# Expert rows scattered by choice and token, read back with plain loads, and summed on TensorE with diagonal matrices

## The reference

```python
    g_p, g_idx = lax.top_k(g_probs, 1)                       # the best of 4 groups
    ...
    e_p, e_idx = lax.top_k(e_probs, TOP_K)                   # the two best of its 8 experts
    e_p = e_p / jnp.sum(e_p, axis=-1, keepdims=True)
    weights = g_p * e_p
    expert_ids = g_idx * EXPERTS_PER_GROUP + e_idx
    ...
    a = jax.nn.silu(jnp.einsum('sd,edf->sef', xs, w_gate)) * jnp.einsum('sd,edf->sef', xs, w_up)
    return jnp.einsum('sef,efd->sd', a * cw[..., None], w_down)
...
        x = x + gt2[:, None, :] * ffn
    ...
    return modulate(rmsnorm(x, norm_f_g), sh_f, sc_f, dt)
```

## Time and profile before

| | us |
|---|---|
| median of 3 runs | 1380.87 |
| lowest, highest | 1378.67, 1381.21 |
| span of the profiled execution | 1383.9 |
| TensorE busy in the span | 1155.6 (84%) |
| VectorE busy | 659.2 (48%) |
| ScalarE busy | 324.7 (23%) |
| GpSimd busy | 138.1 (10%) |

### The profile page before, as it was taken

How to read it: one execution, slowest core, us unless ns; L and a number is a source line. 1 busy time by engine, 2 the same in 40 slices (tenths; PEclk the granted TensorE clock), 3 DMA queues, 4 the chain that set the end, 5 groups by cost and what they waited for, 6 DMA issues and landing times.

```text
span 1383.9 us, 16773 instructions
## 1 busy us (share of the span) xinstructions
PE 1155.6 (84%) x6596; PEld 936.1 (68%) x6596; DVE 659.2 (48%) x1390; ACT 324.7 (23%) x601; POOL 138.1 (10%) x211
## 2 busy tenths in 40 slices
PE   1589969999899989898978999729999999999700
PEld 1367958898789879796965444328888888888500
DVE  3744553362536666766762333462333333333286
ACT  1434261134314453344332111220000000000021
POOL 0000100000000000000000000142111111110083
PEclk9999985589756989999888999868999999999955
DMA  9301420032200513232177342525899898896172
GB/s 344 116 1 31 144 70 0 1 92 66 87 1 0 164 50 110 89 92 77 42 249 285 134 143 92 206 55 172 336 333 334 331 333 334 331 332 257 52 272 86
DMA packets 86861, 216.03 MB, mean 156 GB/s; under 512 B 18400, under 2 KB 47120, under 8 KB 78480
## 3 DMA queue, kind: packets, MB, share of 16 engines
q1 hardware_dynamic: 61152, 148.41, 30.6%
q0 software_dynamic: 13664, 50.26, 11.1%
q10 hardware_dynamic: 11984, 16.54, 3.4%
HBM read 194.70 MB, written 32.93 MB: 164 GB/s over the span
## 4 chain that ended last, share of the span: by engine, by line
PE 73%; DVE 13%; DMA 4%; ACT 4%; issue 2%; ACTq 2%; POOL 0%; POOLq 0%; SPq 0%; DVEq 0%
PE PS L1731 17%; PE PS L1682 8%; PE PS L1738 8%; PE PS L1599 7%; PE PS L1554 7%; PE PS L1555 7%; PE PS L1556 6%; PE PS L1614 2%; DVE X L1488 2%; PE PS L1723 2%; PE PS L1525 2%; PE PS L1616 2%; DMA WF<-in_w_in 2%; PE PS L1602 2%; PE PS L1600 1%
## 5 line engine op out<-in xcount | busy, mean ns | idle before, releaser
L1731 PE MATMUL PS<-XGT,WGU 128*128 128x96 f32 x2048 | 236.8, 277 | 0.0
L1731 PEld LDWEIGHTS PS<-XGT,WGU 128*128 128x128 f32 x2048 | 235.3, 194 | 0.5 <-issue 0.5
L1554 PE MATMUL PS<-WH,HT 128*128 128x256 f32 x512 | 151.8, 297 | 2.6 <-ACT FD L785 1.6
L1555 PE MATMUL PS<-WL,HT 128*128 128x256 f32 x512 | 150.6, 294 | 0.0
L1556 PE MATMUL PS<-WH,HL 128*128 128x256 f32 x512 | 150.4, 294 | 0.0
L1599 PE MATMUL PS<-XL 64*128 64x128 f32 (+1 forms) x640 | 120.9, 356 | 9.3 <-ACT KH L864 5.7
L1599 PEld LDWEIGHTS PS<-XL 64*128 64x128 f32 (+1 forms) x640 | 113.9, 269 | 12.3 <-ACT KH L864 10.9
L1171 DVE COPY_PREDICATED AT<-MASK,PS 128x64 f32<-128x64 uint8 x320 | 72.7, 227 | 100.1 <-PE PS L1602 81.4
L1682 PE MATMUL PS<-WOUT,OT 128*128 128x512 f32 x256 | 113.4, 602 | 3.5 <-DVE H2T L1277 3.3
L1738 PE MATMUL PS<-WDN,ATT 128*96 128x512 f32 x256 | 115.0, 592 | 0.0
L1554 PEld LDWEIGHTS PS<-WH,HT 128*128 128x128 f32 x512 | 104.7, 204 | 3.9 <-DVE WL L1071 2.2
(11 more groups left out here) (258 smaller groups left out, 1652.5 us busy)
## 6 DMA issues: line engine op xcount, KB each, us to landing
WGU<-in_w_exp_gate SPq DMA_DIRECT2D x32, 1024.0 KB, 8.3
WGU<-in_w_exp_up SPq DMA_DIRECT2D x32, 1024.0 KB, 11.1
WDN<-in_w_exp_down SPq DMA_DIRECT2D x32, 1024.0 KB, 5.0
AR<-in_w_ada POOLq DMA_DIRECT2D x32, 512.0 KB, 4.3
WF<-in_w_in SPq DMA_DIRECT2D x28, 512.0 KB, 5.4
expert_rows<-YB ACTq DMA_DIRECT2D x32, 384.0 KB, 8.6
AST<-in_w_ada SPq DMA_DIRECT2D x16, 512.0 KB, 12.2
AR<-in_w_ada_final POOLq DMA_DIRECT2D x16, 512.0 KB, 3.8
```

What stands on the lines that cost most here:

```text
L1554: MM(ps, wh, xh, start=first, stop=False)
L1555: MM(ps, wh, xl, start=False, stop=False)
L1731: last = MM(GU[par][:, col:col + C], WGU[slot][:, m, k, j * P:(j + 1) * P], XGT[:, par, k, :], start=(k == 0), stop=(k == KD - 1))
```

## The change

1. `ys_d` is no longer laid out by expert slot but as planes of rows by token: choice 0 of token j in row j, choice 1 in row 2048 + j (`PLANE` is 2T = 2048). The table holds this row number (`TID` has one column more, for k); its low 11 bits are the token. Empty slots hold 7168, which a bounds check leaves out both as a token number (its low 11 bits are 1024) and as a row.
2. After `IDX` is read, VectorE masks it into `IDXG` (token numbers) in one instruction, and the gathers use that.
3. The stores on ScalarE are gone. GpSimd scatters the 96 rows of `YB` by the column of `IDX` (`scatter`), in its loop ahead of the gather of the expert seven further on.
4. The fill of the extra slices is gone.
5. ScalarE writes 16 diagonal 128x128 matrices `DIAG[k, t]` with the tokens' weights `WPAIR` when the down projection of expert 29 is done.
6. In the last stage SP loads both rows of each token of a tile with one plain DMA of 1 MB, four tiles deep; TensorE makes four 512-column matmuls per tile, which weight and sum the two rows in PSUM; VectorE adds that to `X1`, two tiles ahead of the norm, and adds the shift itself. GpSimd has no part in it.

```diff
-    FILL = -(-NX * C // NT)
+    PLANE = 2 * T
+    PAD = 7 * T
...
-        ys_d = nc.dram_tensor("expert_rows", [NSLOT, D], F32, kind="Internal").ap()
+        ys_d = nc.dram_tensor("expert_rows", [PLANE + T, D], F32, kind="Internal").ap()
...
+            for s in range(2):
+                sp.wait_ge(y_st[s], 16 * NE // 2)
+            sp.wait_ge(extras_done, 1)
+            ys_rows = ys_d.rearrange("(k t p) d -> p k t d", p=P, t=NT)
+
+            def load_rows(t):
+                sp.dma_start(YG[:, t % 4, :, :], ys_rows[:, 0:3:2, t, :]).then_inc(yg_in[t % 4], 16)
+
+            for t in range(4):
+                load_rows(t)
             for t in range(NT):
+                if t + 4 < NT:
+                    sp.wait_ge(ysum_ready, t + 1)
+                    load_rows(t + 4)
                 sp.wait_ge(out_ready, t + 1)
                 sp.dma_start(out_rows[:, t, :], OUTT[:, t % 2, :]).then_inc(out_st[t % 2], 16)
...
-            nc.gpsimd.memset(ZT[:], T).then_inc(zt_ready, 1)
+            nc.gpsimd.memset(ZT[:], PAD).then_inc(zt_ready, 1)
...
-            pool.iota(TID[:], [[P, NT]], base=0, channel_multiplier=1).then_inc(ios, 1)
+            pool.iota(TID[:], [[PLANE, 2], [P, NT]], base=0, channel_multiplier=1).then_inc(ios, 1)
...
-            for t in range(NT):
-                pool.wait_ge(pj_ready, number[("wo", t, 0)] + 1)
-                lo, hi = FILL * t, min(FILL * (t + 1), NX * C)
-                pool.dma_start(ys_d[NE * C + lo:NE * C + hi, :], x[0, 0:hi - lo, :]).then_inc(ys_filled, 16)
...
-            pool.wait_ge(idx_in, 16)
+            pool.wait_ge(idxg_ready, 1)
...
+            def scatter(n, par):
+                pool.wait_ge(y_ev, n + 1)
+                nc.gpsimd.tensor_copy(IDXS[:, par:par + 1], IDX[:, bass.ds(n, 1)]).then_inc(idxs, 1)
+                pool.wait_ge(idxs, n + 1)
+                nc.gpsimd.tensor_tensor(TICK[:], IDENT[:, 0:1], IDENT[:, 0:1], ALU.add)
+                pool.indirect_dma_start(
+                    out=ys_d, out_offset=bass.IndirectOffsetOnAxis(ap=IDXS[:, par:par + 1], axis=0),
+                    in_=YB[0:C, par, :], in_offset=None,
+                    bounds_check=PLANE + T - 1, oob_is_err=False).then_inc(y_st[par], 16)
+
             for s in range(4):
                 gather(0, s, True)
-            with pool.Fori(1, NE // 4) as it:
+            for s in range(4):
+                if s == 3:
+                    scatter(0, 0)
+                gather(1, s, False)
+            with pool.Fori(2, NE // 4) as it:
                 for s in range(4):
+                    scatter(4 * it + (s - 7), (s + 1) % 2)
                     gather(it, s, False)
+            for n in range(NE - 7, NE):
+                scatter(n, n % 2)
...
-            def shift(t):
-                pool.wait_ge(out_scaled, t + 1)
-                nc.gpsimd.tensor_tensor(OUTT[:, t % 2, :], OUTT[:, t % 2, :], SHF[:], ALU.add).then_inc(out_ready, 1)
-
-            for t in range(NT):
-                if t >= 4:
-                    pool.wait_ge(x2_ready, t - 3)
-                for k in range(2):
-                    pool.indirect_dma_start(
-                        out=YG[:, t % 4, k, :], out_offset=None, in_=ys_d,
-                        in_offset=bass.IndirectOffsetOnAxis(ap=SLOT[:, k, t:t + 1], axis=0)).then_inc(yg_in[t % 4], 16)
-                if t >= 4:
-                    shift(t - 4)
-            for t in range(NT - 4, NT):
-                shift(t)
...
-            def store(m, par, row):
-                act.wait_ge(y_ev, m + 1)
-                act.dma_start(ys_d[bass.ds(row, C), :], YB[0:C, par, :]).then_inc(y_st[par], 16)
...
+            act.wait_ge(y_ready, NE - 2)
+            for k in range(2):
+                for t in range(NT):
+                    last = A(DIAG[:, k, t, :], IDENT[:], ACT.Copy, scale=WPAIR[:, k, t:t + 1])
+            last.then_inc(diag_ready, 1)
...
+            v_.wait_ge(idx_in, 16)
+            V.tensor_single_scalar(IDXG[:], IDX[:], PLANE - 1, op=ALU.bitwise_and).then_inc(idxg_ready, 1)
...
             def add_rows(t):
-                for k in range(2):
-                    if k == 0:
-                        v_.wait_ge(yg_in[t % 4], 32 * (t // 4 + 1))
-                    i = V.scalar_tensor_tensor(out=X1[:, t, :], in0=YG[:, t % 4, k, :], scalar=WPAIR[:, k, t:t + 1],
-                                               in1=X1[:, t, :], op0=ALU.mult, op1=ALU.add)
...
+                v_.wait_ge(ysum_ready, t + 1)
+                V.tensor_tensor(X1[:, t, :], X1[:, t, :], YS[t % 2], ALU.add).then_inc(x2_ready, 1)
 
             add_rows(0)
+            add_rows(1)
             for t in range(NT):
-                if t + 1 < NT:
-                    add_rows(t + 1)
+                if t + 2 < NT:
+                    add_rows(t + 2)
...
+                v_.wait_ge(out_scaled, t + 1)
+                V.tensor_tensor(OUTT[:, t % 2, :], OUTT[:, t % 2, :], SHF[:], ALU.add).then_inc(out_ready, 1)
...
+            pe.wait_ge(diag_ready, 1)
+            for t in range(NT):
+                pe.wait_ge(yg_in[t % 4], 16 * (t // 4 + 1))
+                if t >= 2:
+                    pe.wait_ge(x2_ready, t - 1)
+                for half in range(2):
+                    hs = slice(half * HALF, (half + 1) * HALF)
+                    for k in range(2):
+                        last = MM(YS[t % 2][:, hs], DIAG[:, k, t, :], YG[:, t % 4, k, hs], start=(k == 0), stop=(k == 1))
+                last.then_inc(ysum_ready, 1)
```

More of the change, by code:

```diff
@@ L63, in layer_kernel @@
     NSLOT = (NE + NX) * C
-    FILL = -(-NX * C // NT)
+    PLANE = 2 * T
+    PAD = 7 * T
+    assert T & (T - 1) == 0
     GLA_UNITS, HG_UNITS = 2, 4
@@ L321, in layer_kernel @@
         SLOT = at("SLOT", 205.5625, [P, 2, NT], U32)
-        TID = at("TID", 205.625, [P, NT], U32)
+        TID = at("TID", 205.625, [P, 2, NT], U32)
+        IDXG = at("IDXG", 201.0, [C, NE + NX], U32)
         IDX = at("IDX", 200.5, [C, NE + NX], U32)
         IDXC = at("IDXC", 200.75, [C, 4], U32)
+        IDXS = at("IDXS", 200.78125, [C, 2], U32)
         XE = at("XE", 200.8125, [1, NX], I32)
@@ L330, in layer_kernel @@
         OUTT = at("OUTT", 64, [P, 2, D])
+        DIAG = at("DIAG", 136, [P, 2, NT, P])
         PS = ctx.enter_context(nc.psum_tensor("PS", [P, 8 * HALF], F32))
@@ L340, in layer_kernel @@
         YP = [PS[:, (4 + 2 * i) * HALF:(6 + 2 * i) * HALF] for i in range(2)]
+        YS = YP
         xn_d = nc.dram_tensor("xn_rows", [T, D], F32, kind="Internal").ap()
@@ L430, in layer_kernel @@
         extras_done = sem("extras_done")
-        ys_filled = sem("ys_filled")
+        idxs = sem("idxs")
+        idxg_ready = sem("idxg_ready")
+        xidxs = sem("xidxs")
+        diag_ready = sem("diag_ready")
+        ysum_ready = sem("ysum_ready")
         yg_in = [sem(f"yg_in{s}") for s in range(4)]
@@ L610, in _ @@
                             out=tab_d, out_offset=bass.IndirectOffsetOnAxis(ap=SLOTP[:, k, t:t + 1], axis=0),
-                            in_=TID[:, t:t + 1], in_offset=None, bounds_check=NSLOT - 1,
+                            in_=TID[:, k, t:t + 1], in_offset=None, bounds_check=NSLOT - 1,
                             oob_is_err=False).then_inc(table_st, 16)
@@ L631, in gather @@
                     pool.wait_ge(t_ready, 4 * it + (s - 3))
-                nc.gpsimd.tensor_copy(IDXC[:, s:s + 1], IDX[:, bass.ds(4 * it + s, 1)]).then_inc(idxc, 1)
+                nc.gpsimd.tensor_copy(IDXC[:, s:s + 1], IDXG[:, bass.ds(4 * it + s, 1)]).then_inc(idxc, 1)
                 pool.wait_ge(idxc, 4 * it + (s + 1))
@@ L649, in _ @@
                         pool.wait_ge(x_done, 16 * i + 16)
-                        nc.gpsimd.tensor_copy(IDXC[:, 0:1], IDX[:, bass.ds(i + NE, 1)]).then_inc(xidx, 1)
+                        nc.gpsimd.tensor_copy(IDXC[:, 0:1], IDXG[:, bass.ds(i + NE, 1)]).then_inc(xidx, 1)
                         pool.wait_ge(xidx, i + 1)
@@ L656, in _ @@
                             bounds_check=T - 1, oob_is_err=False).then_inc(xxg_in, 16)
-                pool.nop()
-            for s in range(2):
-                pool.wait_ge(y_st[s], 16 * NE // 2)
-            pool.wait_ge(extras_done, 1)
-            pool.wait_ge(ys_filled, 16 * NT)
-            def shift(t):
-                pool.wait_ge(out_scaled, t + 1)
-                nc.gpsimd.tensor_tensor(OUTT[:, t % 2, :], OUTT[:, t % 2, :], SHF[:], ALU.add).then_inc(out_ready, 1)
-            for t in range(NT):
-                if t >= 4:
-                    pool.wait_ge(x2_ready, t - 3)
-                for k in range(2):
-                    pool.indirect_dma_start(
-                        out=YG[:, t % 4, k, :], out_offset=None, in_=ys_d,
-                        in_offset=bass.IndirectOffsetOnAxis(ap=SLOT[:, k, t:t + 1], axis=0)).then_inc(yg_in[t % 4], 16)
-                if t >= 4:
-                    shift(t - 4)
-            for t in range(NT - 4, NT):
-                shift(t)
+                        pool.wait_ge(xyev, i + 1)
```

(19 more changed lines are left out.)

9 lines of the change are left out of this document (1 added, 8 removed).

## The result

The changed kernel takes 1368.95 us, the median of four runs (1367.32 to 1372.58), against 1380.78 for the kernel before on the same chip (1378.67 to 1381.21, four runs): ratio 0.9918, 95% interval 0.99 to 0.9935. The forecast was 1368.6 us, in a range of 1363 to 1377. The number came out; two terms in it did not, and they cancelled.

What follows compares the result with a forecast made beforehand. TensorE was taken to bound the experts, VectorE the last stage. First output 1330.6 + 23.5 + 6.9 = 1361.0, plus 10.3 gives 1371.3, 1371.6 with the index: 12.3 us less, 1380.9 - 12.3 = 1368.6 us, range 1363 to 1377.

Steps and rivals of the forecast that it cites:

- Index, fill, scatter, diagonals: Before the last stage: index mask +0.3 us; fill's removal nothing; scatter hidden, 10 us slack; diagonals hidden, up to 4.4 uncovered.
- rival (c): In the experts: a scatter landing later than 20.5 us holds them up; at 25 us, 55 us slower; chance 0.03.
- rival (d): More than 16 us gained: fill partly held TensorE back (at most 6.5 us), or clock up at once; chance 0.05.
- The hand-over into the last stage: From 1307.7 us: copy to DMA instruction 1.0 us, last scatter's landing 4.0, first load in at 1317.7.
- Rival (b): Last stage: paired-row loads are slow, below about 205 GB/s; 1.7 us slower at 198 GB/s, 29 at 132; chance 0.06.
- The matmuls: Last stage, four per tile: 0.43 us each at full clock, 0.85 at half, so 1.7 or 3.4 us a tile.
- The clock: TensorE's falls to half after the last down projection, back 5 us after work resumes; bounds -3 to +2.2 us.
- The load chain: Last stage: load t+4 waits for output t-1; 8.1 to 9.8 us against 9.4; 0 to +1 us, taken as 0.
- The period: Last stage, VectorE's time per tile: 4.7 us for 6.64, bounded by 4.5 to 5.0.
- The end: From the last shift to the end of the span: 10.3 us, kept unchanged.
- signs of being wrong: A tile over 6 us, VectorE waiting for TensorE or TensorE for loads in the steady part, TensorE gaps in the experts.
- Rival (a): Last stage: loads and matmuls late together, first output at 1336 to 1339 us, gain only 2 to 6; chance 0.12.

Runs made afterwards that it cites:

- kernel 7: The changed kernel with the eight fill writes (8.3 MB) put back on GpSimd's queue, into a tensor nobody reads; 1369.28 us, ratio 0.9904 to the kernel before.
- kernel 8: The changed kernel with each expert's scatter issued twice, the second into a second tensor; 1372.34 us, ratio 0.9925 to the kernel before.
- kernel 4: The changed kernel with twelve dummy 512-column matmuls on TensorE between the last down projection and the first expert rows; 1367.49 us, ratio 0.989 to the kernel before.
- kernel 6: The changed kernel without diagonals and tail matmuls: VectorE makes the two weighted adds from the plainly loaded rows; 1366.54 us, ratio 0.9902 to the kernel before.
- Kernel 5: The changed kernel with eight row buffers in place of four, all eight loads issued at once; 1367.36 us, ratio 0.9907 to the kernel before.
- kernel 1: The kernel before with only the shift moved from GpSimd to VectorE; 1368.06 us, ratio 0.9897 to the kernel before.
- kernel 2: The changed kernel with the shift put back on GpSimd; 1377.06 us, ratio 0.9959 to the kernel before.
- kernel 3: The changed kernel with one more one-column GpSimd instruction after the last output is ready; 1373.68 us, ratio 0.9942 to the kernel before.
- kernel 9: The changed kernel with tiles 0 and 1 summed on VectorE, eight row and four output buffers, shift before next add, 16 dummy matmuls; 1359.72 us, ratio 0.9846.

## Why the prediction came out, and where it was wrong

**Index, fill, scatter, diagonals: right.** GpSimd's first index copy came 183.87 us after the output projection's start, 183.58 before: 0.29 us later, forecast 0.3.

```profile
924.01 0.19 DVE L1430 TENSOR_SCALAR IDXG<-IDX 96x53 uint32<-96x53 uint32 x1 [2.72 <-DMA IDX<-slot_tokens]
924.26 0.18 POOL L650 COPY IDXC<-IDXG 96x1 uint32<-96x1 uint32 x1 [4.98 <-DVE IDXG L1430]
```

That delay does not reappear at the end of the experts (561.8 us after, 561.9 before); so its price in the sum is inside the spread of 0.6 us. Fill and scatter are shown to cost nothing by kernels 7 and 8, which also rules out rival (c) and the fill's part in rival (d). In the changed kernel all scatters, and the loads behind them, land in 11.4 us or less, where rival (c) needed over 20.5. The diagonals were done at 1300.4, before the last down projection ended at 1302.2.

**The hand-over into the last stage: right.** Forecast 1.0 + 4.0 + 5.0 = 10.0 us from the last evacuation to the first rows; measured 1303.5 to 1313.5, 10.0. By the rule of the Trainium skill (DMA: Bandwidth & Descriptors, in Anatomy of one DMA — SWDGE) the prediction had estimates of 2.6 us for the scatter and 4.4 for a load; this case's traces have 3.62 and 5.24, nearer to the rows it went by. That rule is for DMAs issued by GpSimd, as the scatter is; the load is issued by SyncE. (The two estimates lie 2.0 us under the prediction's own terms, not 1.9; and tile 1, with its numbers, would have ended at 1323.7 and not 1324.0. Neither slip matters here.) Rival (b) is out: the loads of paired rows move 406 to 420 GB/s in the rows of kernel 4's section, more than the earlier trace rows have. The rule of the Trainium skill behind that rival (DMA: Bandwidth & Descriptors, in Latency and other measured facts) speaks of rows 4 or 8 MiB apart from partition to partition; no run here has such a stream, and a pair 8 MB apart in each partition does no harm.

**The matmuls: wrong by a factor of two.** This is the step that failed. The prediction read "3.44 us for 8" as eight matmuls of 512 columns and took 0.43 us each, four a tile (the earlier trace rows show the same price, 6.88 us for 16). Those were eight instructions of four matmuls. The right price is 0.86 us at full clock and 1.7 at half: 3.43 us each for tiles 1 and 2, and 6.5 for tile 0 (1313.6 to 1320.1), which ran at half clock nearly to its end, where 1.7 and 3.4 were forecast. The clock itself went about as forecast: 0.50 at first, 0.69 on average in 1318 to 1320 and so back to full 5 to 6 us after work resumed. With that, tile 2 is ready 23.5 us after the last evacuation and not 18.1, and the first output 28.1 and not 22.9: +5.2 us. Kernels 4 and 6 show from two sides what TensorE's part costs ahead of the first output: with full clock from the start it is 2.8 us less (26.6 after the last down projection for 29.4), without TensorE 7.2.

**The load chain: the same error again.** It was taken as 0 to +1 with 3.4 us for the matmuls at half clock. TensorE had waited 4.04 us for the rows of tile 5, its clock was at half (columns as in the earlier trace rows), and the tile took 6.3 us: +3.5.

```profile
1338.00:1340.00 2.00, 2.00 (x3) 0.97 (x4) 1.92 (x3) 0.91 (x4) 0.00 (x0) 0.50 0.94 268
1340.00:1342.00 2.00, 2.00 (x3) 0.75 (x3) 0.74 (x1) 0.00 (x0) 0.00 (x0) 0.50 0.97 391
```

Kernel 5 takes that wait away and has 3.5 us less. The period was 4.55 us for 4.7, and the last two tiles took a little longer, -0.5 over the stage. Together +3.0.

**The end: wrong, on the other side.** "10.3 us lie from there to the end of the span; I keep them." Nothing in the prediction asked what they were. 3.1 of them are the last output; the other 7.2 are GpSimd's drain, which hangs behind GpSimd's last instruction and went with the shift. Kernels 1, 2 and 3 show it by taking it away, and by bringing 4 us of it back. What sets its length stays open: it ends 10.2 us after GpSimd's last instruction in the kernel before and 12.0 in kernel 1, 6.9 in kernels 2 and 3, 7.5 with the fill put back (kernel 7), 9.5 with twice the scatters (kernel 8).

The sum: +5.2 + 3.0 - 7.2 = +1.0 us on the forecast tail of 64.9 (from 1306.4 to 1371.3); measured 66.0. The forecast was met by luck, since the errors cancelled. The bounds did not cover them: +5.2 us stood against at most +2.2 for the clock, +3.5 against 0 to +1 for the load chain, and the end had no bound at all. Two of the prediction's own signs of being wrong came true as well: VectorE waited for TensorE and TensorE for a load at tile 5, and the first output came 29.4 us after the last down projection, not 22 to 25.

**The rivals.** Rival (a) asked for late loads, which did not come, but its time of the first output, 1336 to 1339 on the clock of the kernel before, was nearly met by another way: 29.4 us after the last down projection is 1335.8 there. Had the 10.3 us stayed, the change would have gained 4.3 us, in (a)'s span of 2 to 6. The 0.12 it had was too little for a case that only the unseen drain kept from deciding.

The reasoning named the right cause for the gain only in part. It put the whole gain on the shorter period. The period did fall, from 6.64 to 4.55 us, and mostly by the sum: kernel 1, with the shift's move alone, has 5.93, kernel 2, with the sum's alone, 4.34. But what the sum gave per tile it took back ahead of the first output and at tile 5, while the shift's move also took the drain off the end. On the whole tail the shift's move alone does better than all parts together: kernel 1 is 2.4 us ahead of the changed kernel.

## What to carry to other kernels

Before pricing an operation from a row, compare the row's count with the program's: here an fp32 matmul is two instructions, and the "x8" were four. Ask of every stretch of a tail which engine ends it, the time behind the last useful instruction too, and let GpSimd finish early: here a drain of 7 to 12 us followed its last instruction. And when a change has several parts, run the cheapest part alone; here one moved instruction gave all of it, and the part that went to TensorE first paid in kernel 9, where the first tiles stayed on VectorE and the loads no longer waited (its parts were not all tried singly).

## What the runs showed that I had not expected

- GpSimd's closing drain: from the end of its last instruction to the end of the drain 10.2 us (kernel before), 12.0 (kernel 1), 6.8 to 6.9 (changed kernel, kernels 2 and 3), 7.5 (kernel 7), 9.5 (kernel 8). It costs only what outlasts the rest: 7.2 us in the kernel before, 4.0 and 4.3 in kernels 2 and 3, nothing in the others.
- A VectorE instruction on 128x1 elements took 2.34 us beside a GpSimd addition of 2.34 us over three SBUF operands, and 0.16 without one (kernel 2). The shift on GpSimd thus held more than the second add of the kernel before (3.24 us for 1.28). VectorE's sum of an SBUF and a PSUM operand wasn't held: 1.22 us beside such an addition and 1.22 without.
- Dummy matmuls that end 1.08 us before the real ones kept the clock at full; with 2.88 us between them it fell to half during the real ones (kernels 4 and 9).
- Executions of one kernel differ by 2 to 8 us here (1354.4 to 1362.7 for the combined one). Between the profiled ones, one per kernel, the stretch from the output projection to the end of the experts doesn't differ; its start wanders by 5.6 us. That this is what spreads the times of one kernel is likely, but not shown. Two kernels of this kind are better compared from a common event in their traces than by single times.
